# Second-stage convolved projections in fp32r parts with three banks, and a mixer output turned tile by tile

## The chip, the cores and the metric

The kernel runs on one core of one Trainium2 chip (trn2). The metric is device microseconds from start to end of one launch; the table further down gives the median of several. All stages follow one another inside this launch: five engines (TensorE, VectorE, ScalarE, GpSimd, SyncE) run their own instruction queues and meet at semaphores.

## The reference

256 tokens of width 1024 pass through two stacks. The first has two layers, each of feed-forward, hybrid mixer, feed-forward:

```python
for l in range(DEPTH):                        # DEPTH = 2
    h = swiglu(rms_norm(x, ...), w_gate, w_up, w_down); x = x + 0.5 * rms_norm(h, ...)
    h = hybrid_mixer(rms_norm(x, ...), ...);            x = x + rms_norm(h, ...)
    h = swiglu(rms_norm(x, ...), ...);                  x = x + 0.5 * rms_norm(h, ...)
# inside hybrid_mixer: sparse attention (its blocks are xb below: keys plus a position code),
# a short convolution u = cg * xc, and at the end
merged = concatenate([rms_norm(attn, ...), rms_norm(conv, ...)]); return merged @ w_out
```

The second has one layer. Its first step projects a context `hc` and the tokens `h` (both 256 x 1024), and runs a convolution of 5 taps and a silu over the projected channels:

```python
pc = hc @ w_in[:, :OFF_CF]
xb_c = silu(dwconv_centred(pc[..., :XB_CH], conv_w[:, :XB_CH], conv_b[:XB_CH]))
dtc = softplus(pc[..., OFF_DT:OFF_CF] + dt_bias)
p = h @ w_in
xl = silu(dwconv_centred(p[..., :XB_CH], ...)); cl = silu(dwconv_centred(p[..., OFF_CF:OFF_Z], ...))
```

Then come a state-space scan, a Fourier mix, gates, and a mixture of 32 experts over all tokens.

## The kernel before

**Products.** In the first stack and from the scan on, a product of fp32 numbers is made of three fp32r products: the weights and the inputs are each split into a high part (rounded to fp32r) and a low part (the rest), and hi·hi, hi·lo and lo·hi are added up in a bank of PSUM. The weights come in chunks through a ring of three slots of 128x4096, filled by transfers that SyncE issues in the order in which the chunks are used. A chunk is split in two halves of 128x2048. ScalarE writes a half's high part into one of four buffers (`act_split`, a CAST at L381), VectorE the low part into `ring_lo` (`dve_split`, a TENSOR_TENSOR at L390), and TensorE waits for both. A slot is filled again when TensorE has used the halves in it (`half_used`).

**The second stage's projections** (`pe_projections`, `act_projections`, `dve_projections`, about 1088 us to 1320 us) are the exception. They consist of 56 blocks `n` of 128 channels; blocks 0 to 23 are of the context, the rest of the tokens. The weights stay whole (fp32): four blocks share a chunk of 512 channels, and a block is 8 matmuls of 128x256 (L1780), which the profile counts as 16. The results go to bank `n % 2`. For each block VectorE takes the first tap and the bias out of PSUM (L1829), then adds four taps (L1834); ScalarE applies silu (L1804); TensorE turns the block (two transposes, L1794), and ScalarE copies the turned block out of PSUM (L1819). Eight of the 56 (kind C) are not turned. TensorE starts block `n` when the taps of block `n - 2` are done:

```python
pe.wait_ge(*(at("tap", n - 2) if n >= 2 else at("hout", self.before, 0, n)))
for k in range(KD):
    mm = pe.matmul(bank[n % 2][:, 0:SEQ], w[:, k, j * P:(j + 1) * P], self.conv_src(n)[:, k, :], ...)
```

Around the blocks stand: `pe_dt(0)` ahead of block 0 and `pe_dt(1)` ahead of block 24 (the step widths `dt`, 32 small matmuls, L1845); `act_softplus` ahead of ScalarE's part of blocks 0 and 24 (L1863 to L1869, two of its steps with a table load of their own); `pe_cumsum` behind blocks 1 and 25 (L1856, L1857); the normed and turned tokens `x1` at blocks 1 to 7 (L1745 and others); and `dve_xw_ctx` at blocks 14, 18, 22 and 26 (L1961, eight 128x512 products by twos for each). The high part of the tokens (`hx`) is made by ScalarE at block 50, the low part by VectorE behind block 55 (L2034).

**The last feed-forward of the first stack** ends with its down projection and the joint (`act_joint`, `dve_joint`, L641, L665, L671), which adds the normed result to `x`. The projections' block 0 waits there for `hout`, the point where VectorE has read banks 0 and 1.

**The mixers** run twice (for layer 0 from about 200 us to 362 us). `xb` is made on VectorE (L1486, 8 operations) behind `dve_u` (L1538) and `dve_max` (L1409, L1412), and TensorE's `pe_compress` (L1167) waits for it. At the end, the attention's output `o` is scaled (L1528 for tile 1, L1531 for tile 0), turned in two halves of four channel blocks with both tiles in each (`pe_turn_o`, `act_turn_half`, `dve_turn_half`, L1399), and multiplied by the last two halves of `w_out` (`pe_last`, L415). The joint and the next feed-forward's first turns (L608) follow.

## Time and profile before

| what | us |
|---|---|
| median of 3 runs | 2609.37 (2603.39 to 2612.96) |
| the profiled execution, its own time | 2603.46 |
| span of its core in the profile | 2602.0 |
| mean granted clock of TensorE | 0.995 of full speed |
| TensorE busy | 98% of the span |
| VectorE, ScalarE, GpSimd busy | 42%, 33%, 4% |
| experts (about 1650 us to the end), TensorE's work | over a third of the span |

The busy shares are of the whole span. Stages differ: in the experts VectorE and ScalarE have a tenth of the time to do, in the first stack and the projections half of it or more. "Own time" is what was measured for the execution that was profiled; it is 5.9 us below the median of the runs. Times below that look like `1138.72` are microseconds from the start of the span.

### The profile page before, as it was taken

The numbers are of one execution on the slowest core, as the hardware profiler recorded it, in microseconds if no ns is written. First come the engines' busy times: TensorE is split into PE (matmuls) and PEld (weight loads), VectorE is DVE, ScalarE is ACT, GpSimd is POOL, SyncE is SP. The second block draws the span as 40 slices with busy tenths as digits, with TensorE's granted clock in tenths as the row PEclk, the third lists the DMA queues.
The fourth block names the chain that finished last, engine by engine and source line by source line (L and its number), as shares of the span: only waits on it lengthen the run. The fifth ranks groups of instructions, "written<-read, shape, count | busy, mean of one in ns | idle before, by whom it ended". The sixth has DMA issues, their size and how long they took to land.

```text
span 2602.0 us, 31966 instructions
## 1 busy us (share of the span) xinstructions
PE 2554.2 (98%) x13032; PEld 1712.8 (66%) x13032; DVE 1093.5 (42%) x1710; ACT 854.0 (33%) x1357; POOL 100.5 (4%) x139
## 2 busy tenths in 40 slices
PE   8999999999999999999999999999999999999998
PEld 6888678888887688888878878544444444444443
DVE  5545565555464655476665636311111111111111
ACT  5435454444454454323144644211111111111111
POOL 1000210000002100000000000000000000000000
PEclk9999999999999999999999999999999999999999
DMA  7556655555565665424322336899999999999996
GB/s 261 180 175 208 239 204 190 182 198 181 175 216 196 233 223 186 158 102 158 134 81 82 113 119 212 322 425 430 431 431 431 431 431 431 431 431 432 431 431 257
DMA packets 69389, 688.45 MB, mean 265 GB/s; under 512 B 7906, under 2 KB 8050, under 8 KB 11920
## 3 DMA queue, kind: packets, MB, share of 16 engines
q1 hardware_dynamic: 66368, 676.27, 66.4%
q0 software_dynamic: 2928, 10.87, 1.3%
q8 instruction: 67, 1.10, 0.2%
q14 instruction: 26, 0.21, 0.0%
HBM read 683.98 MB, written 1.05 MB: 263 GB/s over the span
## 4 chain that ended last, share of the span: by engine, by line
PE 96%; DVE 2%; ACT 1%; DMA 0%; issue 0%; POOL 0%; SPq 0%; DVEq 0%; ACTq 0%
PE bank L415 39%; PE bank L2748 26%; PE bank L1780 7%; PE bank L2695 4%; PE bank L2762 2%; PE bank L2738 2%; PE bank L452 1%; PE bank L2113 1%; PE bank L2091 1%; PE bank L720 1%; PE bank L1045 1%; PE bank L1167 1%; DVE ring_r L390 1%; PE bank L1237 1%; PE bank L1016 1%; PE bank L455 1%
## 5 line engine op out<-in xcount | busy, mean ns | idle before, releaser
L390 DVE TENSOR_TENSOR ring_r<-ring,split_r 128x2048 fp32r<-128x2048 f32 (+1 forms) x200 | 451.6, 2284 | 340.5 <-ACT split_r L381 340.3
L415 PE MATMUL bank<-split_r,xT_r 128*128 128x512 f32 (+1 forms) x1760 | 548.0, 389 | 6.4 <-DVE xT_r L1399 5.4
L381 ACT CAST split_r<-ring 128x2048 fp32r<-128x2048 f32 (+1 forms) x200 | 375.1, 1902 | 153.2 <-PE bank L415 124.2
L415 PE MATMUL bank<-split_r,work_r 128*128 128x512 f32 x1280 | 409.6, 396 | 0.5 <-DVE ring_r L390 0.5
L415 PEld LDWEIGHTS bank<-split_r,xT_r 128*128 128x128 f32 x1760 | 330.2, 189 | 75.7 <-DVE xT_r L1399 5.8
L2748 PE MATMUL bank<-ring,work 128*64 128x512 f32 x1536 | 342.1, 594 | 1.7 <-DVE work L2712 1.7
L415 PE MATMUL bank<-ring_r,xT_r 128*128 128x512 f32 (+1 forms) x880 | 340.4, 387 | 0.0
L415 PEld LDWEIGHTS bank<-split_r,work_r 128*128 128x128 f32 x1280 | 240.3, 188 | 54.3 <-issue 3.3
L2748 PEld LDWEIGHTS bank<-ring,work 128*64 128x64 f32 x1536 | 107.1, 137 | 228.6 <-issue 228.6
L415 PE MATMUL bank<-ring_r,work_r 128*128 128x512 f32 x640 | 249.2, 389 | 0.0
L2748 PE MATMUL bank<-split,work 128*64 128x512 f32 x1024 | 232.2, 595 | 0.0
L1780 PE MATMUL bank<-work,ring 128*128 128x256 f32 x896 | 200.9, 379 | 0.0
L415 PEld LDWEIGHTS bank<-ring_r,xT_r 128*128 128x128 f32 x880 | 166.2, 189 | 32.2
L1780 PEld LDWEIGHTS bank<-work,ring 128*128 128x128 f32 x896 | 166.9, 190 | 23.1 <-issue 1.0
L2785 ACT ACTIVATE work<-work 128x512 f32<-128x512 f32 x32 | 20.1, 629 | 467.5 <-DVE work L2796 467.5
L2748 PEld LDWEIGHTS bank<-split,work 128*64 128x64 f32 x1024 | 70.5, 137 | 130.2 <-issue 128.0
L415 PEld LDWEIGHTS bank<-ring_r,work_r 128*128 128x128 f32 x640 | 120.3, 188 | 27.8 <-issue 4.1
L2695 PE MATMUL bank<-work 128*128 128x64 f32 x1056 | 121.7, 274 | 0.5 <-DVE work L2719 0.5
L2695 PEld LDWEIGHTS bank<-work 128*128 128x128 f32 x1056 | 120.5, 192 | 0.7 <-DVE work L2719 0.7
L2798 DVE TENSOR_SCALAR work<-bank 128x512 f32<-128x512 f32 x32 | 22.1, 691 | 234.6 <-PE bank L2762 234.6
L2748 PE MATMUL bank<-work 128*64 128x512 f32 x512 | 115.3, 592 | 0.0
L2796 DVE TENSOR_SCALAR work<-bank 128x512 f32<-128x512 f32 x32 | 22.1, 691 | 217.8 <-PE bank L2762 217.8
(369 smaller groups left out, 2281.8 us busy)
## 6 DMA issues: line engine op xcount, KB each, us to landing
ring<-in_stream SPq DMA_DIRECT2D x256, 1024.0 KB, 5.0
ring<-in_stream SPq DMA_DIRECT2D x96, 2048.0 KB, 14.0
split<-in_stream SPq DMA_DIRECT2D x64, 2048.0 KB, 13.5
work<-in_stream SPq DMA_DIRECT2D x32, 2048.0 KB, 11.3
row<-in_rows POOLq DMA_DIRECT2D x6, 512.0 KB, 4.4
ring<-in_stream SPq DMA_DIRECT2D x4, 560.0 KB, 4.6
work<-in_conv POOLq DMA_DIRECT2D x2, 768.0 KB, 5.8
x<-in_x SPq DMA_DIRECT2D x1, 1024.0 KB, 10.1
```

The lines of the kernel that those rows point to most:

```text
L381: act.copy(hi, self.part(half, self.ring)).then_inc(*up("half_hi", half.h))
L390: dve.tensor_tensor(self.part(half, self.ring_lo), self.part(half, self.ring), hi.bitcast(F32), ALU.subtract).then_inc(*up("half_lo", half.h))
L415: mm = self.nc.tensor.matmul(out, a[x][a_at], w[y][w_at], start=start and n == 0, stop=stop and n == 2)
L452: pe.matmul(out, self.xT[0][:, 4 * j + k, tokens], w[y][:, k], start=4 * j + k + y == 0, stop=False)
L455: mm = pe.matmul(out, self.xT[1][:, 4 * j + k, tokens], w[0][:, k], start=False, stop=4 * j + k == KD - 1)
L720: tr = pe.transpose(self.bank[b][:, j * SEQ + m * P:j * SEQ + (m + 1) * P], self.hid[i % 2][:, m, (j2 + j) * P:(j2 + j + 1) * P], self.ident)
L1016: mm = pe.matmul(bank[2 * (i % 2) + hh % 2][:, c0:c0 + P], self.qT[1][r, h // 2, m * P:(m + 1) * P], self.kT[r, 2 * b + g, kb * P:(kb + 1) ...
L1780: mm = pe.matmul(bank[n % 2][:, 0:SEQ], w[:, k, j * P:(j + 1) * P], self.conv_src(n)[:, k, :], start=(k == 0), stop=(k == KD - 1))
L2695: mm = pe.matmul(bank[k // 4][:, k * SLOTS:(k + 1) * SLOTS], self.xs[:, m, k * P:(k + 1) * P], self.Pm[:, m, :], start=(m == 0), stop=(m = ...
L2738: mm = self.nc.tensor.matmul(self.bank[4 + 2 * m + h][:, :], self.PT[rows, m * P:(m + 1) * P], self.yb[rows, :], start=False, stop=stop)
L2748: mm = self.nc.tensor.matmul(self.bank[bank][h * SLOTS:(h + 1) * SLOTS, :], lhsT(k0 + k), w[:, k, h * 512:(h + 1) * 512], start=start and ...
L2762: mm = pe.matmul(bank[part][h * SLOTS:(h + 1) * SLOTS, :], self.sel[0:N_EXP, :], self.bias[0:N_EXP, part * D + h * 512:part * D + (h + 1) ...
```

## The change

There are two parts. In **the projections of the second stage**, the 56 blocks take their weights and their inputs in high and low parts: 24 matmuls of 128x256 a block instead of 8, all fp32r. The chunks of weights are laid out so that one half holds two blocks, so 28 halves more pass through `act_split` and `dve_split`, one at every even `n`. The context is split too (`act_context_hi`, `dve_context_lo`), during the last feed-forward, and `hx` now at blocks 13 and 15. The blocks go to three banks, and TensorE waits for the taps of block `n - 3`. The first tap moves from VectorE to ScalarE (`act_conv_first`). `pe_dt(0)` moves into the last feed-forward's `pe_last`, and `pe_dt(1)` from block 24 to block 12.

In **the mixers**, `xb` is made ahead of `dve_u` and `dve_max`, and the output is turned one tile of tokens at a time, tile 1 first; the joint and the next feed-forward take tile 1 first as well.

```diff
         x_c, dt_c, bf_c, cf_c, bb_c, cb_c = [n_mod + c for c in range(4)], *(n_mod + c for c in range(4, 9))
-        for c in (dt_c, bf_c, bb_c, *x_c, dt_c, bf_c, cf_c, bb_c, cb_c, *x_c):
+        for i, c in enumerate((dt_c, bf_c, bb_c, x_c[0], dt_c, *x_c[1:], bf_c, cf_c, bb_c, cb_c, *x_c)):
             w = 2 * NH2 if c == dt_c else 512
-            self.add_chunk(t["stream2"][c, :, 0:KD * w], KD, w, False)
-        self.n_slots = RING - 1
+            self.add_chunk(t["stream2"][c, :, 0:KD * w], KD, w, c != dt_c, c != dt_c)
+            self.n_slots = RING - 1
+        self.first_piece = len(self.halves)
...
         if split:
             n = 2 if kt * width > HALF else 1
             for j in range(n):
-                half = Half(len(self.halves), kt // n, width, chunk, j)
+                half = Half(len(self.halves), kt if by_column else kt // n, width // n if by_column else width, chunk, j)
...
         if self.last_ffn:
             self.dve_split(3)
             self.dve_context_turned()
-            self.dve_split(KF // 2 - 5)
+            self.dve_split(KF // 2 - 7)
+            self.dve_context_lo()
+            self.dve_split(2)
         else:
             self.dve_split(KF // 2 - 2)
...
@@ -1099,10 +1113,8 @@
             if i >= 2:
                 self.pe_mod_turn(st, i - 2)
         self.pe_out_u(st, 1)
-        self.pe_turn_o(st)
-        for j in range(2):
-            pe.wait_ge(*at("turn_lo", (st, "o"), j))
-        self.out_done = self.pe_last(self.xT, 0, st, lambda k: None)
+        self.out_done = self.pe_last(self.xT, 0, st, lambda m, k: None if k else ("turn_lo", (st, "o"), m),
+                                     lambda: self.pe_turn_o(st, 0))
...
+            elif i == 7:
+                self.act_split(2)
             if i == 3:
                 act.wait_ge(*at("conv", st))
                 act.wait_ge(*at("zeroed", st, 3))
                 self.act_rstd((st, "u"), self.u, 512, 6)
...
-        for m, col in ((1, 5), (0, 4)):
-            act.wait_ge(*at("o", st, m))
-            act.wait_ge(*self.s.last("sum_sq"))
-            act.activation(self.squares[:, 0:512], self.o[:, m, :], ACT.Square, scale=512 ** -0.5,
-                           accum_out=self.stat[:, col:col + 1]).then_inc(*up("sum_sq", (st, "o"), m))
-            self.act_split(1)
-        self.act_turn_half((st, "o"), 0)
+        self.act_o_squares(st, 0)
+        self.act_turn_o(st, 1)
+        self.act_turn_o(st, 0)
         self.act_split(2)
         self.act_joint(st, self.out_done, 1.0)
...
@@ -1470,12 +1519,6 @@
         dve.wait_ge(*last("att_step"))
         dve.reciprocal(self.gates, self.gates).then_inc(*up("att_step"))
 
-        dve.wait_ge(*at(*self.xc_done))
-        dve.wait_ge(*at("z", st, 3, 1))
-        self.dve_u(st, 0)
-        self.dve_u(st, 1)
-        self.dve_max(st, 1)
-        self.dve_max(st, 0)
         dve.wait_ge(*at("kc2", st, 1))
         dve.wait_ge(*at("zeroed", st, 3))
         for kv in range(2):
@@ -1486,6 +1529,12 @@
                     i = dve.tensor_tensor(self.xb[kv][:, 8 * jh:8 * jh + 8, g, 0:N_CMP], v[:, :, jh:jh + N_CMP, 0],
                                           spread(pe_cols[:, 8 * jh:8 * jh + 8], 2, N_CMP), ALU.add)
         i.then_inc(*up("xb", st))
+        dve.wait_ge(*at(*self.xc_done))
+        dve.wait_ge(*at("z", st, 3, 1))
+        self.dve_u(st, 0)
+        self.dve_u(st, 1)
+        self.dve_max(st, 1)
+        self.dve_max(st, 0)
...
+            if i == 7:
+                self.dve_o_scaled(st, 1)
+                self.dve_split(2)
...
-        dve.wait_ge(*at("rstd", (st, "o"), 1))
-        dve.tensor_scalar(self.o[:, 1, :], self.o[:, 1, :], self.stat[:, 5:6], None, ALU.mult).then_inc(*up("o_scaled", st, 1))
-        self.dve_split(1)
-        dve.wait_ge(*at("rstd", (st, "o"), 0))
-        dve.tensor_scalar(self.o[:, 0, :], self.o[:, 0, :], self.stat[:, 4:5], None, ALU.mult).then_inc(*up("o_scaled", st, 0))
-        self.dve_split(1)
-        self.dve_turn_half((st, "o"), 0)
+        self.dve_turn_o(st, 1)
+        self.dve_o_scaled(st, 0)
+        self.dve_turn_o(st, 0)
         self.dve_split(2)
...
     def conv_src(self, n):
-        return self.src[0] if n < 24 else self.src[1]
+        return self.cx if n < 24 else self.hx
+
+    def conv_bank(self, n):
+        return self.bank[(0, 1, 4)[n % 3]]
 
     def conv_turns(self, n):
         return self.blocks[n][0] != "C"
 
     def conv_at(self, n):
 
-        return self.raw_at(self.conv_chunk[n]) if self.blocks[n][2] == 3 else self.s.at("conv_mm", n)
+        return self.s.at("half_used", self.conv_half[n]) if n % 2 else self.s.at("conv_mm", n)
...
-        pe.wait_ge(*(at("tap", n - 2) if n >= 2 else at("hout", self.before, 0, n)))
+        pe, at, up = self.nc.tensor, self.s.at, self.s.up
+        if n % 2 == 0:
+            self.conv_now = self.pe_take()
+        half, w = self.conv_now
+        self.conv_half[n] = half.h
+        if n >= 2:
+            pe.wait_ge(*(at("tap", n - 3) if n >= 3 else at("cx_lo", 0)))
+        else:
+            pe.wait_ge(*at("hout", self.before, 0, n))
+        if n == 8:
+            pe.wait_ge(*at("turn_even", "x1", 1))
...
+        x, cols = self.conv_src(n), slice(n % 2 * P, (n % 2 + 1) * P)
         for k in range(KD):
-            mm = pe.matmul(bank[n % 2][:, 0:SEQ], w[:, k, j * P:(j + 1) * P], self.conv_src(n)[:, k, :],
-                           start=(k == 0), stop=(k == KD - 1))
-        mm.then_inc(*(self.raw_up(ch.c) if j == 3 else up("conv_mm", n)))
+            for i, (y, z) in enumerate(((0, 0), (0, 1), (1, 0))):
+                mm = pe.matmul(self.conv_bank(n)[:, 0:SEQ], w[y][:, k, cols], x[z][:, k, :], start=k == 0 and i == 0,
+                               stop=k == KD - 1 and i == 2)
+        mm.then_inc(*(up("half_used", half.h) if n % 2 else up("conv_mm", n)))
         if n >= 2 and self.conv_turns(n - 2):
             self.pe_conv_turn(n - 2)
...
+    def act_conv_first(self, n):
+        act, at, up = self.nc.scalar, self.s.at, self.s.up
+        wt = self.conv_w[:, self.blocks[n][3]]
+        act.wait_ge(*self.conv_at(n))
+        if n >= 3:
+            act.wait_ge(*at("conv_turned" if self.conv_turns(n - 3) else "conv_silu", n - 3))
+        act.activation(self.acc[n % 3], self.conv_bank(n)[:, 0:SEQ], ACT.Identity, scale=wt[:, 2:3],
+                       bias=wt[:, 5:6]).then_inc(*up("tap_first", n))
+
...
@@ -1821,16 +1909,13 @@
     def dve_conv(self, n):
         dve, at, up, last = self.nc.vector, self.s.at, self.s.up, self.s.last
         kind, a, j, block = self.blocks[n]
-        acc, src, wt = self.acc[n % 3], self.bank[n % 2], self.conv_w[:, block]
-        dve.wait_ge(*self.conv_at(n))
-        if n >= 3:
-            dve.wait_ge(*(at("conv_turned", n - 3) if self.blocks[n - 3][0] in ("Bc", "Xc", "X")
-                          else at("conv_silu", n - 3)))
-        dve.tensor_scalar(acc, src[:, 0:SEQ], wt[:, 2:3], wt[:, 5:6], ALU.mult, ALU.add).then_inc(*up("tap"))
+        acc, src, wt = self.acc[n % 3], self.conv_bank(n), self.conv_w[:, block]
+        dve.wait_ge(*at("tap_first", n))
         for tap in (0, 1, 3, 4):
             s = tap - 2
             to = acc[:, max(0, -s):SEQ - max(0, s)]
-            dve.wait_ge(*last("tap"))
+            if tap:
+                dve.wait_ge(*last("tap"))
             dve.scalar_tensor_tensor(to, src[:, max(0, s):SEQ - max(0, -s)], wt[:, tap:tap + 1], to, ALU.mult,
...
     def pe_projections(self):
         pe, at = self.nc.tensor, self.s.at
-        pe.wait_ge(*at("turn_even", "ctx", 5))
-        pe.wait_ge(*at("turn_odd", "ctx", 7))
-        self.pe_dt(0)
         for n in range(56):
-            if n == 24:
+            if n == 12:
                 pe.wait_ge(*at("turn_even", "x1", 5))
                 pe.wait_ge(*at("turn_odd", "x1", 7))
...
+            self.act_conv_first(n)
+            if n:
+                self.act_conv(n - 1)
+            if n >= 3 and self.conv_turns(n - 3):
+                self.act_conv_turn(n - 3)
+            if n % 2 == 0:
+                self.act_split(1)
...
+            elif n == 13:
+                act.wait_ge(*at("turn_odd", "x1", 7))
                 act.copy(self.hx[0], self.src[1]).then_inc(*up("hx_hi", 0))
...
                 self.dve_dt_raw(n // 24)
             self.dve_conv(n)
+            if n % 2 == 0:
+                self.dve_split(1)
             if n in (0, 24):
                 self.dve_dt_step(n // 24)
...
-        dve.wait_ge(*at("hx_hi", 0))
-        dve.tensor_tensor(self.hx[1], self.src[1], self.hx[0].bitcast(F32), ALU.subtract).then_inc(*up("hx_lo", 0))
+            elif n == 15:
+                dve.wait_ge(*at("hx_hi", 0))
+                dve.wait_ge(*self.raw_at(self.dt_chunk[1]))
+                dve.tensor_tensor(self.hx[1], self.src[1], self.hx[0].bitcast(F32), ALU.subtract).then_inc(*up("hx_lo", 0))
```

(The layout of the weights, which the host writes, puts two times 256 channels behind one another. The renamed banks of `pe_dt`, the moves of `z`, and the ring's sync in the experts are left out here.)

On SyncE, which issues the transfers, the second stage's chunks began like this before:

```order
L348 DMA ring<-in_stream 128x512 [waits raw_used]
L348 DMA ring<-in_stream 128x2048 [waits raw_used] x16
```

and begin like this now:

```order
L347 DMA ring<-in_stream 128x512 [waits half_used]
L353 DMA ring<-in_stream 128x2048 [waits half_used] x2
L353 DMA ring<-in_stream 128x2048 [waits raw_used] x2
L353 DMA ring<-in_stream 128x2048 [waits half_used] x2
```

(the 128x512 is the weights of the second `dt`; before it the same stood for the first). A transfer now waits for a half's use by its own slot's last chunk. The stage has two slots instead of three, since the third holds the tokens; in the planner's order the chunk of blocks 12 to 15 goes into the slot of blocks 8 to 11, and so its halves wait for those of blocks 8, 9 and 10, 11.

On ScalarE, among the blocks that are turned, this stood before (line, operation, output <- input, what it waits for):

```order
L1804 ACTIVATE work<-work 128x256 [waits second_dve]
L1819 COPY work<-bank 128x2x128 [waits second_pe]
```

and this stands there now, for two blocks (the piece repeats):

```order
L1884 ACTIVATE work<-bank,work 128x256 [waits second_pe]
L1892 ACTIVATE work<-work 128x256 [waits second_dve]
L1907 COPY work<-bank 128x2x128 [waits second_pe]
L380 CAST split_r<-ring 128x2048 [waits half_used,dma_ring1_1]
L1884 ACTIVATE work<-bank,work 128x256 [waits second_pe,half_used]
L1892 ACTIVATE work<-work 128x256 [waits second_dve]
L1907 COPY work<-bank 128x2x128 [waits second_pe]
L1884 ACTIVATE work<-bank,work 128x256 [waits second_pe]
L1892 ACTIVATE work<-work 128x256 [waits second_dve]
```

L1884 is the first tap, which was VectorE's; L1892 is the silu of the block before it, L1907 the turned block of two earlier still. The CAST of a half stands behind them once in two blocks. On VectorE, at the same place, before:

```order
L1829 TENSOR_SCALAR work<-bank,work 128x256 [waits second_pe]
L1834 SCALAR_TENSOR_TENSOR work<-bank,work 128x254 [waits second_dve]
L1834 SCALAR_TENSOR_TENSOR work<-bank,work 128x255 [waits second_dve] x2
L1834 SCALAR_TENSOR_TENSOR work<-bank,work 128x254 [waits second_dve]
```

and now, again for two blocks:

```order
L1919 SCALAR_TENSOR_TENSOR work<-bank,work 128x254 [waits second_act]
L1919 SCALAR_TENSOR_TENSOR work<-bank,work 128x255 [waits second_dve] x2
L1919 SCALAR_TENSOR_TENSOR work<-bank,work 128x254 [waits second_dve]
L389 TENSOR_TENSOR ring_r<-ring,split_r 128x2048 [waits half_hi]
L1919 SCALAR_TENSOR_TENSOR work<-bank,work 128x254 [waits second_act]
L1919 SCALAR_TENSOR_TENSOR work<-bank,work 128x255 [waits second_dve] x2
L1919 SCALAR_TENSOR_TENSOR work<-bank,work 128x254 [waits second_dve]
```

The first tap is gone from VectorE; its four taps wait for ScalarE's, and a subtraction that waits for the CAST of the same half (`half_hi`) stands between two blocks. At the end of a mixer VectorE had this:

```order
L1528 TENSOR_SCALAR work<-work,stat 128x512 [waits rms_pool]
L390 TENSOR_TENSOR ring_r<-ring,split_r 128x2048 [waits half_hi]
L1531 TENSOR_SCALAR work<-work,stat 128x512 [waits rms_pool]
L390 TENSOR_TENSOR ring_r<-ring,split_r 128x2048 [waits half_hi]
L1399 SCALAR_TENSOR_TENSOR xT_r<-bank,cols,xT_r 128x256 [waits turn_hi]
L1399 SCALAR_TENSOR_TENSOR xT_r<-bank,cols,xT_r 128x256
L1399 SCALAR_TENSOR_TENSOR xT_r<-bank,cols,xT_r 128x256 [waits turn_hi]
L1399 SCALAR_TENSOR_TENSOR xT_r<-bank,cols,xT_r 128x256
L390 TENSOR_TENSOR ring_r<-ring,split_r 128x2048 [waits half_hi] x2
L665 TENSOR_TENSOR work<-bank,row 128x512 [waits post_sq,dma_row]
```

and has this now:

```order
L1418 SCALAR_TENSOR_TENSOR xT_r<-bank,cols,xT_r 128x128 [waits turn_hi]
L1418 SCALAR_TENSOR_TENSOR xT_r<-bank,cols,xT_r 128x128 x3
L1425 TENSOR_SCALAR work<-work,stat 128x512 [waits rms_pool]
L1418 SCALAR_TENSOR_TENSOR xT_r<-bank,cols,xT_r 128x128 [waits turn_hi]
L1418 SCALAR_TENSOR_TENSOR xT_r<-bank,cols,xT_r 128x128 x3
L389 TENSOR_TENSOR ring_r<-ring,split_r 128x2048 [waits half_hi] x2
L668 TENSOR_TENSOR work<-bank,row 128x512 [waits post_sq,dma_row]
```

The scaling of tile 1 and two subtractions have moved ahead of this piece, into the attention's last unit, and the turned output (now L1418) comes by tiles; the last two subtractions still stand right ahead of the joint (L665, now L668).

## Rows read from the trace of the kernel before

**Rows 1.** The page's first part: busy time, share of the span, instructions.

```profile
PE 2554.2 (98%) x13032; PEld 1712.8 (66%) x13032; DVE 1093.5 (42%) x1710; ACT 854.0 (33%) x1357; POOL 100.5 (4%) x139
```

**Rows 2.** Windows: span, busy PE, PEld, DVE, ACT, POOL, clock, DMA share, GB/s.

```profile
1088.00:1320.00 232.00, 228.97 (x1119) 195.08 (x1117) 159.17 (x327) 68.74 (x149) 8.26 (x11) 1.00 0.35 133
264.00:268.00 4.00, 3.34 (x20) 1.56 (x22) 2.06 (x4) 4.00 (x6) 0.59 (x1) 0.70 0.49 114
350.90:354.30 3.40, 2.75 (x7) 2.20 (x8) 3.02 (x4) 2.70 (x2) 0.00 (x0) 0.51 0.24 99
```

**Rows 3.** Timeline of one projection block: start, us, engine, line, idle before.

```profile
1138.72 0.54 DVE L1829 TENSOR_SCALAR work<-bank,work 128x256 f32<-128x256 f32 x1 [1.06 <-PE bank L1780]
1138.74 3.62 PE L1780 MATMUL bank<-work,ring 128*128 128x256 f32 x16
1138.94 0.37 ACT L1819 COPY work<-bank 128x256 f32<-128x256 f32 x1 [0.83 <-PE bank L1794]
1139.30 2.04 DVE L1834 SCALAR_TENSOR_TENSOR work<-bank,work 128x254 f32<-128x254 f32 x4
1141.37 0.42 ACT L1804 ACTIVATE work<-work 128x256 f32<-128x256 f32 x1 [2.06 <-DVE work L1834]
1142.42 3.62 PE L1780 MATMUL bank<-work,ring 128*128 128x256 f32 x16
```

**Rows 4.** The page's fifth part: groups of the two splits and of weight loads.

```profile
L390 DVE TENSOR_TENSOR ring_r<-ring,split_r 128x2048 fp32r<-128x2048 f32 (+1 forms) x200 | 451.6, 2284 | 340.5 <-ACT split_r L381 340.3
L381 ACT CAST split_r<-ring 128x2048 fp32r<-128x2048 f32 (+1 forms) x200 | 375.1, 1902 | 153.2 <-PE bank L415 124.2
L415 PEld LDWEIGHTS bank<-split_r,xT_r 128*128 128x128 f32 x1760 | 330.2, 189 | 75.7 <-DVE xT_r L1399 5.8
```

**Rows 5.** Chain and timeline: fp32r matmuls of 280 and of 256 columns.

```profile
227.08 6.16 PE bank L415 x48
1644.57 1.68 PE L2531 MATMUL bank<-work_r 128*128 128x256 f32 x12
```

**Rows 6.** Lines by form, window 1088 to 1318 us, VectorE and ScalarE.

```profile
L1961 DVE TENSOR_TENSOR work<-work 128x512 f32<-128x512 f32 x16 | 9.9, 683 | 0.0
...
L1804 ACT ACT_TABLE_LOAD x4 | 5.1, 1283 | 0.1
```

**Rows 7.** Timeline of the projections' start and end.

```profile
1086.62 1.34 DVE L665 TENSOR_TENSOR work<-bank,row 128x512 f32<-128x512 f32 x2 [15.54 <-ACT work L641]
1088.36 3.68 PE L1845 MATMUL bank<-ring,work 128*128 128x64 f32 x32
1092.38 0.28 DVE L1884 TENSOR_TENSOR work<-bank,work 128x128 f32<-128x128 f32 x1
1092.70 0.31 ACT L1863 ACTIVATE work<-work 128x128 f32<-128x128 f32 x1 [2.74 <-DVE work L1884]
1098.23 0.42 ACT L1804 ACTIVATE work<-work 128x256 f32<-128x256 f32 x1 [0.53 <-DVE work L1834]
1318.82 0.42 ACT L1804 ACTIVATE work<-work 128x256 f32<-128x256 f32 x1 [2.06 <-DVE work L1834]
```

**Rows 8.** The page's sixth part: transfers, KB each, us from issue to landing.

```profile
ring<-in_stream SPq DMA_DIRECT2D x256, 1024.0 KB, 5.0
```

**Rows 9.** TensorE's waits: us in total, times, longest.

```profile
PE bank L1167 <- DVE work L1486: 7.4, 2, 3.7
PE bank L415 <- DVE xT_r L1399: 5.4, 2, 2.7
```

**Rows 10.** Timeline of the first mixer, around xb and around its end.

```profile
266.54 5.57 DVE L390 TENSOR_TENSOR ring_r<-ring,split_r 128x2048 fp32r<-128x2048 f32 x2 [1.94 <-ACT split_r L381]
276.12 0.50 PE L415 MATMUL bank<-split_r,xT_r 128*128 128x512 f32 x1
351.83 4.49 DVE L390 TENSOR_TENSOR ring_r<-ring,split_r 128x2048 fp32r<-128x2048 f32 x2 [0.38 <-ACT split_r L381]
359.43 1.34 DVE L665 TENSOR_TENSOR work<-bank,row 128x512 f32<-128x512 f32 x2 [3.10 <-ACT work L641]
```

180 lines of the change are left out of this document (118 added, 62 removed).

## The prediction

> **What bounds the kernel now.** I began with the page's first part and with windows by stage. TensorE is busy 98% of the whole [rows 1], so in the mean only work taken off TensorE, or its waits, can count; but a stage can change hands. In the projections TensorE is busy 228.97 of 232.00 us, VectorE 159.17 and ScalarE 68.74, at full clock [rows 2]. A timeline of one block then shows the order: a block starts every 3.68 us [rows 3], of which 3.62 are its sixteen matmul records; VectorE needs 0.54 + 2.04 and waits 1.06 for TensorE; ScalarE needs 0.42 + 0.37. TensorE sets the pace there, and the other two follow. The reader should see that the slack is 1.1 us on VectorE and 2.9 on ScalarE for each block. In the mixers I read TensorE's waits: two rows stand out that the change touches, 3.7 us for `xb` and 2.7 us for the turned output, once in each of two mixers [rows 9].
>
> **TensorE's side of the projections.** The new block has 24 fp32r matmuls of 256 columns. Forty-eight of 280 columns took 6.16 us, 0.128 each, so 0.117 for 256; twelve of exactly 256 columns took 1.68, 0.140 each with the pipeline's end [rows 5]. I take 0.118: 24 are 2.84, and with the turns (3.68 − 3.46 = 0.22, where 3.46 is the period without turns) 3.06. That is 0.6 us less than now. Over 56 blocks it would be 35 us, if TensorE went on setting the pace. A load of weights is on record with 0.189 [rows 4]; if none lay beside a matmul, a block would take 24 × (0.118 + 0.189) = 7.4. The 0.128 and 0.140 are whole matmuls with their loads, so they speak against that. [...]
>
> **What is added.** One half now holds two blocks. A half costs ScalarE a cast of 1.902 us and VectorE a subtraction of 2.284 [rows 4], 28 times each. ScalarE also gets the first tap: bounded by 0.37 (a copy of 128x256 out of PSUM) and 0.54 (VectorE's) [rows 3]; I take 0.50, since it has a scale and a bias. VectorE gives 0.54 away.
>
> **The pace after it.** Sums per pair of blocks: TensorE 6.1; VectorE 2 × 2.04 + 2.29 = 6.4; ScalarE 2 × (0.50 + 0.42 + 0.37) + 1.90 = 4.5. None of these is the pace, because the queues hook into each other. In the new order ScalarE's cast stands behind the silu of block n − 1 and a copy, and the silu waits for the taps of n − 1. VectorE's subtraction waits for that cast, and the taps of n + 1 stand behind the subtraction. So from the end of one odd block's taps to the next: silu 0.42, copy 0.37, cast 1.90, subtraction 2.29, four taps 2.04, and hand-overs (1141.37 − 1139.30 − 2.04 = 0.03 each, four to five) 0.13. Sum **7.15 us a pair, 3.58 a block**. The taps of block n lie beside the cast (2.04 of 0.42 + 0.37 + 1.90 + 0.06 = 2.75, VectorE waits about 0.7). Before, a pair took 7.36. The whole gain of the fp32r matmuls shrinks to 0.2 us a pair, and TensorE waits a microsecond in each.
>
> **The start.** Before, block 0's taps ended at 1098.2 [rows 7]. Now `pe_dt(0)` (3.5 us of the 3.68 [rows 7], moved, not saved) stands inside the feed-forward's last product, so TensorE is through that at 1092.0 instead of 1088.4. VectorE has the context's low part (2.28, as a half of the same shape [rows 4]) and two subtractions (4.6) ahead of the joint: with `dt` there at about 1086.6, it is free at 1093.5. The joint takes 1092.4 − 1086.6 = 5.8 less 0.4 of waiting (now the squares are done), up to 1099.0; `dt`'s bias 0.3; then ScalarE's softplus 3.7 (1092.70 to 1096.40, two table loads of 1.28 in it), which stood beside matmuls and now stands ahead of the first tap; first tap 0.5; taps 2.04. Block 0's taps end at 1105.7: **+7.5**.
>
> **From there to the last taps.** Before 1318.8 − 1098.2 = 220.6 [rows 7]. Now 27.5 pairs × 7.15 = 196.6. To this I add what doesn't fit in the pair's 0.7 of slack, by following the four queues block after block with these durations (the same hand count for the order of before ends at 1319.1, the trace at 1318.8):
> - blocks 0 to 8: `pe_cumsum(0)`, behind the late softplus, stands ahead of block 2; two further table loads (1.28 [rows 6]) and the squares of x: +9.0;
> - blocks 8 to 12: the transfer. The half of blocks 12, 13 can't be issued before block 9's matmuls end, since it goes into that slot; it lands 5.0 us later [rows 8], then come its cast and subtraction, which VectorE's queue waits for although block 10's taps could go. Twice, 7 + 5 less the slack: +10.6;
> - blocks 14 to 22: two `dve_xw_ctx` (a quarter of 9.9 each [rows 6]) and the tokens' low part 2.28, on VectorE, which had room before: +7.4;
> - blocks 22 to 30: two more `xw` 5.0, the second softplus with 4.2 ahead of block 24's first tap, and the cumsum that waits for it ahead of block 26's matmuls, with two table loads behind, 8.1: +17.3;
> - the rest −0.9 (in the blocks of kind C there is no turn).
>
> Together 240.0: **+19.4**. TensorE's waits also cost clock: after a wait of 2.7 us the window's granted clock is 0.51 over 3.4 us, after the 3.7 us one 0.70 over 4 us [rows 2], so 1.2 to 1.7 us each. In the new stage there are four or five waits of 4 to 9 us, by my count: **+6.5**. Behind the stage, unit 0 gets the tokens' low part (2.28) and the first split earlier: **−1**. Projections: 7.5 + 19.4 + 6.5 − 1 = **+32.4**. With all durations 10% off, the stage's end moves from 1334 to 1351.
>
> **The mixers.** `xb`: TensorE's wait of 3.7 goes, with the 1.2 of clock. But VectorE's two subtractions, from 266.54 to 272.11, end no sooner than ScalarE's casts allow; the product that needs them (276.12) can move to 272.15 at best [rows 10]. **−4.0** each (bounds 0 and −5.5). Output: TensorE's wait of 2.7 and its slow stretch (1.6) go. Then the joint is late next: its first operation stands at 359.43 behind 3.1 us of waiting, and VectorE's two subtractions (from 351.83, 4.5 us) now stand behind the eight smaller turns, and end at about 358.8 [rows 10]. **−1.0** each (bounds −4.3 and +2). Two mixers: **−10** (0 to −20).
>
> **Sum.** 32.4 − 10 = 22.4, less 1 for feed-forwards whose first tile comes earlier: 21.4 by the execution's own 2603.5, so 2625. The median of the runs is 5.9 above that execution: **2631**. What this kernel's measurement can tell from no change is 0.5%, 13 us.
>
> **The rivals.**
> - *The mixers give all.* With both waits and both slow stretches gone, −10 a mixer: 32.4 − 20 − 1 = +11, 2621. For it: the waits are plain in rows 9. Against: VectorE's subtractions in rows 10.
> - *The cast hides.* If ScalarE reached the cast before the taps end (it has 2.6 us of slack a pair), VectorE alone would set 6.45 a pair. 27.5 × 0.7 = 19 less, and with a queue that runs ahead the dips (6.5) and a part of the transfer's wait (some 4) less: 32.4 − 19 − 10 − 10 − 1 = −8, 2602. For it: all sums per engine allow it. Against: the silu ahead of the cast waits for taps.
> - *TensorE stays the pace* (the other side). If splits ran two halves ahead all the time, 3.06 a block: 56 × 0.6 = −35, with the mixers −45, 2564. It decides as soon as the pair's chain is under 6.1. For it: the halves have four buffers, and the second stage's VectorE was 31% idle. Against: 6.4 of VectorE's own work a pair is more than 6.1 already.
> - *Weight loads don't overlap*: 7.4 a block, 56 × 3.7 = +207 less the mixers' 10, 2806. Against: rows 5. [...]
>
> **Chances.** Forecast 0.60, full mixers 0.13, hidden cast 0.12, TensorE 0.10, loads 0.03; 0.02 for others. The likeliest one's own range is 2618 to 2645. The range of 8 in 10 leaves TensorE and the loads out, and reaches from the hidden cast, 2602, to the upper end, 2646. Slower than +13 us (2622) comes with most of the forecast and the loads, 0.60; within 13 us with the full mixers and most of the hidden cast, 0.26; faster with TensorE and the rest of it, 0.14.
>
> **What would show it.** The first taps would start every 3.6 us in pairs of uneven length, and VectorE's subtraction would wait for ScalarE's cast some 0.7 us in each; TensorE would have a wait of a microsecond for each pair, on the low part or on taps. At blocks 0, 10, 12, 24 and 26 waits of 4 to 9 us. Block 0's silu at about 1096 to 1098 after the mixers' 10 are taken off, the last one near 1342. In the mixers L1167's wait is gone, and the matmuls behind it start 4 us sooner. I would be wrong if ScalarE's first tap took 0.8 instead of 0.5 (+8 in all), if the transfer's wait is not there, or if the subtractions ran ahead of the taps.

## The result and the profile after

| what | before | after |
|---|---|---|
| median of 4 runs | 2609.64 (2603.39 to 2612.96) | 2635.24 (2633.54 to 2636.84) |
| own time of the profiled execution | 2603.46 | 2635.03 |
| span | 2602.0 | 2633.7 |

The ratio is 1.0102, 95% interval 1.0088 to 1.0116: the change made the kernel slower by 1.0%. Forecast were 2631 and slower by more than 0.5%. The page's first part answers to [rows 1]:

```profile
PE 2546.0 (97%) x13480; PEld 1723.0 (65%) x13480; DVE 1128.8 (43%) x1691; ACT 930.1 (35%) x1450; POOL 100.7 (4%) x139
```

TensorE has 8 us less to do and takes 32 us longer for it. Windows over the projections, which now last from about 1081 to 1349 us (columns as in [rows 2]), say where:

```profile
1081.00:1110.00 29.00, 20.66 (x123) 19.16 (x122) 18.63 (x24) 16.23 (x25) 5.13 (x6) 0.82 0.41 146
1130.00:1170.00 40.00, 32.87 (x260) 32.13 (x258) 23.57 (x37) 18.62 (x33) 0.00 (x0) 0.91 0.37 130
1230.00:1265.00 35.00, 29.96 (x186) 26.26 (x186) 21.40 (x37) 17.45 (x29) 0.00 (x0) 0.82 0.21 67
1300.00:1340.00 40.00, 36.90 (x303) 36.03 (x304) 35.37 (x54) 24.23 (x41) 4.11 (x4) 1.00 0.47 159
```

TensorE was busy 99% there before, at full clock; now it is idle 3 us in 40 where the stage runs steadily, and 5 to 8 us in 29 to 40 where it doesn't, with the granted clock down to 0.82. What it waits for stands in the view of its waits (us in total, times, longest):

```profile
PE bank L1875 <- ACT work L1907: 20.7, 14, 4.9
PE bank L610 <- DMA x<-in_x: 12.5, 1, 12.5
PE bank L1941 <- DVE work L1982: 10.8, 2, 6.4
PE bank L610 <- DVE x L674: 6.5, 2, 3.3
PE bank L2028 <- DVE work L2046: 5.8, 3, 3.0
```

L1875 is the turn of a block, which stands for the turned copy (L1907) of an earlier one; L1941 is the cumsum behind softplus; L610 are the first turns of `x` for a feed-forward, a wait that has taken the place of the one for the turned output. The two of [rows 9] are gone.

The chain that ended last, cut to one steady pair of blocks (start, us, what; pieces under 0.1 us are left out but the silu's), shows the pace:

```profile
1306.69 0.22 issue
1306.90 0.35 ACT work L1907
1307.26 1.82 ACT split_r L380
1309.10 2.29 DVE ring_r L389
1311.39 0.40 DVE work L1919
1311.82 0.49 DVE work L1919
1312.34 0.49 DVE work L1919
1312.86 0.49 DVE work L1919
1313.37 0.03 ACT work L1892
1313.48 0.22 issue
1313.70 0.35 ACT work L1907
```

No piece of TensorE is in it. It reads: copy, cast, subtraction, four taps, silu (L1892), and again. The silu's piece is short because the rest of it stands as "issue": its record starts at 1306.58, and its 0.42 overlap the copy's start. One round takes 1313.70 − 1306.90 = 6.80 us. The trap of the transfer at block 10 stands in the timelines of VectorE and ScalarE:

```profile
1139.18 2.04 DVE L1919 SCALAR_TENSOR_TENSOR work<-bank,work 128x254 f32<-128x254 f32 x4
1148.52 2.29 DVE L389 TENSOR_TENSOR ring_r<-ring,split_r 128x2048 fp32r<-128x2048 f32 x1 [7.30 <-ACT split_r L380]
1150.73 3.98 DVE L1919 SCALAR_TENSOR_TENSOR work<-bank,work 128x254 f32<-128x254 f32 x8
1161.63 2.29 DVE L389 TENSOR_TENSOR ring_r<-ring,split_r 128x2048 fp32r<-128x2048 f32 x1 [6.92 <-ACT split_r L380]
```

```profile
1146.59 1.90 ACT L380 CAST split_r<-ring 128x2048 fp32r<-128x2048 f32 x1 [6.88 <-DMA ring<-in_stream]
1159.70 1.90 ACT L380 CAST split_r<-ring 128x2048 fp32r<-128x2048 f32 x1 [6.22 <-DMA ring<-in_stream]
```

VectorE stands 7 us for a cast that itself stands for its transfer, twice. At the end of the first mixer (VectorE and TensorE, answering to [rows 10]) the joint is late:

```profile
355.68 4.50 DVE L389 TENSOR_TENSOR ring_r<-ring,split_r 128x2048 fp32r<-128x2048 f32 x2 [0.67 <-ACT split_r L380]
360.09 1.28 DVE L668 TENSOR_TENSOR work<-bank,row 128x512 f32<-128x512 f32 x2
```

```profile
362.09 1.12 PE L610 MATMUL bank<-consts,x 128*128 128x128 f32 x4 [3.25 <-DVE x L674]
```

### The profile page after: what moved, and what is told of

Its sections match the earlier page's. It is cut to its first block, busy times and chain, and to the rows that moved or that the text cites. A ratio compares the mean times of both kernels' runs of the same rounds, so it can differ in the third digit from the quotient of the medians.

```text
span 2633.7 us, 32981 instructions
## 1 busy us (share of the span) xinstructions
PE 2546.0 (97%) x13480; PEld 1723.0 (65%) x13480; DVE 1128.8 (43%) x1691; ACT 930.1 (35%) x1450; POOL 100.7 (4%) x139
## 4 chain that ended last, share of the span: by engine, by line
PE 88%; DVE 6%; ACT 4%; issue 1%; DMA 1%; POOL 0%; SPq 0%; ACTq 0%; DVEq 0%
PE bank L414 38%; PE bank L2840 25%; PE bank L2787 4%; DVE ring_r L389 3%; PE bank L2854 2%; PE bank L2830 2%; PE bank L1861 2%; ACT split_r L380 2%; PE bank L452 1%; DVE work L1919 1%; PE bank L2186 1%; PE bank L2208 1%; PE bank L729 1%; PE bank L1059 1%; PE bank L2028 1%
## 5 line engine op out<-in xcount | busy, mean ns | idle before, releaser
L389 DVE TENSOR_TENSOR ring_r<-ring,split_r 128x2048 fp32r<-128x2048 f32 (+1 forms) x228 | 515.5, 2284 | 370.6 <-ACT split_r L380 370.4
L380 ACT CAST split_r<-ring 128x2048 fp32r<-128x2048 f32 (+1 forms) x228 | 428.6, 1903 | 180.7 <-PE bank L414 120.3
L414 PE MATMUL bank<-split_r,work_r 128*128 128x512 f32 x960 | 301.7, 392 | 0.5 <-DVE ring_r L389 0.5
L414 PEld LDWEIGHTS bank<-split_r,work_r 128*128 128x128 f32 x960 | 180.8, 188 | 38.3 <-DVE ring_r L389 0.9
L414 PE MATMUL bank<-ring_r,work_r 128*128 128x512 f32 x480 | 187.3, 390 | 0.0
L1919 DVE SCALAR_TENSOR_TENSOR work<-bank,work 128x254 f32<-128x254 f32 x224 | 106.5, 481 | 37.9 <-ACT work L1884 31.8
L2879 ACT COPY work<-bank 128x256 f32<-128x256 f32 x32 | 11.9, 372 | 286.2 <-PE bank L2861 286.2
L414 PE MATMUL bank<-split_r,ring_r 128*128 128x512 f32 x320 | 109.0, 412 | 0.0
```

The lines of the kernel that those rows point to most:

```text
L380: act.copy(hi, self.part(half, self.ring)).then_inc(*up("half_hi", half.h))
L389: dve.tensor_tensor(self.part(half, self.ring_lo), self.part(half, self.ring), hi.bitcast(F32), ALU.subtract).then_inc(*up("half_lo", half.h))
L414: mm = self.nc.tensor.matmul(out, a[x][a_at], w[y][w_at], start=start and n == 0, stop=stop and n == 2)
L1919: dve.scalar_tensor_tensor(to, src[:, max(0, s):SEQ - max(0, -s)], wt[:, tap:tap + 1], to, ALU.mult, ALU.add).then_inc(*(up("tap", n) if t ...
```

## The experiments

Each is an edit of the changed kernel if nothing else is said. "Last taps" are those of block 55; where two traces are compared, they are counted from block 0's taps. Two measures are used: the median of the runs, and the trace of one execution.

### The two parts apart

`p_only` puts the mixers back, `m_only` is the kernel before with the mixers' part, `xb_only` the kernel before with this alone:

```diff
+        (xb: 8 operations of VectorE, then_inc xb)
         dve.wait_ge(*at(*self.xc_done))
         dve.wait_ge(*at("z", st, 3, 1))
         self.dve_u(st, 0)
...
         self.dve_max(st, 0)
-        (xb)
```

> The projections' part of the change alone, with the mixers as before. Theory: the parts add up; the changed kernel is at 2635.2 and the mixers' part alone gave 9, so 2642 to 2645 (the prediction's own term for the projections was +32.4, which is 2642). Rival: the mixers and the projections are coupled, through the tile order and the joint, and this runs at 2635 to 2639.

> The kernel before with the mixers' part of the change alone (xb sooner, output tile by tile, tile 1 first); the projections stay fp32 in two banks. My theory, from the changed kernel's trace: xb gives 3.9 us a mixer, the output about 1.4 up to the next feed-forward's first turn, and the low clock behind TensorE's new wait of 3.3 us for the joint takes 1.6 back, so some 3.7 a mixer and up to 7.4 in all, or 2.5 if the first mixer again loses 5 to a low clock: 2601 to 2607 by the median of the runs. Rival, the term of the prediction: 10 us for both, 2600. Second rival: the mixers' part is worth nothing or costs, and all of the 26 us is not the projections' alone: 2610 or more.

> The kernel before with xb ahead of dve_u and dve_max, and nothing else. Theory, the prediction's term: TensorE's wait of 3.7 us goes, and the matmuls that need VectorE's two subtractions start 3.8 to 4.0 us sooner in each mixer, 8 in all: 2601. The output's new order is then worth about 1 for the two mixers (the mixers' part alone ran at 2599.9). Rival: the wait moves on in full to the subtractions, and xb gives under 4 in all: 2605 or more, and the output's order is worth 5.

Measured, with the ratio to the kernel before:

| kernel | median | ratio, 95% interval |
|---|---|---|
| `p_only` | 2639.54 | 1.0119 (1.0102 to 1.0136) |
| `m_only` | 2599.91 | 0.9973 (0.9961 to 0.9984) |
| `xb_only` | 2603.05 | 0.9984 (0.9975 to 0.9994) |

The projections cost 30.6 us (2639.54 − 2608.9), the mixers give 9.1 (2609.0 − 2599.91). The prediction had 32.4 and 10. My revised reading before the run, that the mixers give at most 7.4, fell. `p_only` lies between its theory (from 2642) and its rival (up to 2639), nearer to the rival. The sum is 21.5 and the whole change 25.6, so 4 us are left over. The three intervals are 3 to 4 us wide to each side, so this may be no more than their spread, and the clock in the mixers is another place where it can lie (last section); a coupling of the two parts isn't shown. Of the 9.1, `xb` gives 6.0, between its theory (8) and its rival (under 4). The output's new order is worth 3.1 by the medians, with intervals that overlap. By the traces, from the start of the product with `w_out`'s second half of the convolution's rows to the next feed-forward's second chunk of gate and up weights, it is worth nothing: 35.4 us before (granted clock 0.95), 35.5 in `m_only`, and 34.1 in `xb_only`, whose clock was 1.00 there. Which of the two holds stays open.

### Is TensorE's work what counts? `t_less`

```diff
-            for i, (y, z) in enumerate(((0, 0), (0, 1), (1, 0))):
+            for i, (y, z) in enumerate(((0, 0), (1, 0))):
```

> The changed kernel with two of the three fp32r products of the 56 blocks (the product of the weights' high part with the inputs' low part is left out), all splits, casts and waits as they are. That takes 56 x 8 x 0.12 = 54 us of work off TensorE. Theory (the chain of silu, copy, cast, subtraction and taps sets the pace, TensorE only waits in it): under a tenth of it shows, where TensorE's blocks stand behind the cumsum or a transfer, 2628 to 2637. Rival: TensorE still sets much of the pace, and 20 us or more come off: 2615 or less.

2625.89, 9.3 us less, for an estimated 54 us of work. From block 32's last tap to block 54's it took 1334.0 − 1260.2 = 73.8 us here and 1342.8 − 1269.0 = 73.8 in the changed kernel: the same. VectorE's timeline in it has the waits of the changed kernel:

```profile
1314.05 2.29 DVE L389 TENSOR_TENSOR ring_r<-ring,split_r 128x2048 fp32r<-128x2048 f32 x1 [0.60 <-ACT split_r L380]
1316.26 3.98 DVE L1919 SCALAR_TENSOR_TENSOR work<-bank,work 128x254 f32<-128x254 f32 x8
1320.85 2.43 DVE L389 TENSOR_TENSOR ring_r<-ring,split_r 128x2048 fp32r<-128x2048 f32 x1 [0.61 <-ACT split_r L380]
```

So TensorE isn't the pace in the steady part at all, as forecast. The 9 us come from ahead of block 30 (8.7 by the traces, 3.5 of them in blocks 22 to 30), where TensorE follows a cumsum or a transfer; that is more than the 7 at most that I expected.

### The chain and the transfer: `e_cast`, `e_slot`, `c_slotcast`

`e_cast` moves the cast:

```diff
             self.act_conv_first(n)
+            if n % 2 == 0:
+                self.act_split(1)
             if n:
                 self.act_conv(n - 1)
             if n >= 3 and self.conv_turns(n - 3):
                 self.act_conv_turn(n - 3)
-            if n % 2 == 0:
-                self.act_split(1)
```

> The changed kernel with one move: ScalarE's cast of a half stands ahead of the silu and the turned copy instead of behind them. Theory (the pair of blocks is a chain silu, copy, cast, subtraction, taps): the cast no longer waits for taps, the pair falls from 6.8 to 7.1 us to VectorE's own sum of 6.3, and VectorE's waits for the cast go where the weights are there; at blocks 8 to 12 the silu now stands behind the cast that waits for its transfer, which takes some of it back. Net 5 us sooner at the last taps, about 2630. Rival: VectorE's or TensorE's own work is already the pace, and a pair stays at 6.8: no change, 2635.

2635.21, no change, where 5 us less were expected. The theory of the pace held all the same: blocks 32 to 54 took 1341.1 − 1273.0 = 68.1 us instead of 73.8, 6.2 a pair instead of 6.7. But the price at the transfer was larger than I had put it: from block 10's taps to block 12's 21.7 us instead of 13.1, and from block 8's to block 12's 37.9 instead of 26.6. ScalarE's timeline shows why:

```profile
1144.37 1.90 ACT L380 CAST split_r<-ring 128x2048 fp32r<-128x2048 f32 x1 [7.50 <-DMA ring<-in_stream]
1146.17 0.41 ACT L1892 ACTIVATE work<-work 128x256 f32<-128x256 f32 x1
...
1152.49 0.56 ACT L1884 ACTIVATE work<-bank,work 128x256 f32<-128x256 f32 x1 [4.62 <-PE bank L1861]
1160.28 1.90 ACT L380 CAST split_r<-ring 128x2048 fp32r<-128x2048 f32 x1 [7.22 <-DMA ring<-in_stream]
```

The silu (L1892) and the copy (L1907) are stuck behind the waiting cast, TensorE's turn waits 7.6 us for that copy, and the next transfer's slot only comes free when TensorE goes on. `e_slot` takes that wait away; the second `dt`'s weights go into the unused half of the third slot (in the planner's loop, with the same offset in the transfer and in `pe_take_raw`):

```diff
+            if i == 4:
+                chunk = Chunk(len(self.chunks), t["stream2"][c, :, 0:KD * w], KD, w, 2, self.in_slot[2])
+                chunk.at_half = 1
...
+                continue
```

> The changed kernel with the weights of the second dt in the free half of the third slot, so that the weights of blocks 12 to 15 go into the slot of blocks 4 to 7 and are issued after block 5 instead of block 9. Theory (the transfer sets the pace at blocks 8 to 12): ScalarE's two casts there, which stood 6.9 and 6.2 us for the transfer, no longer wait, and the last taps end 11 us sooner, 2624. Rival: the wait only hid another one, as for the low parts or the state products behind it, and under 4 us come out: 2631 or more.

2620.31: 14.9 less, where 11 were expected; by the traces 231.5 us from the first taps to the last instead of 244.9, 13.4 less. The cast at the same place:

```profile
1144.75 0.42 ACT L1902 ACTIVATE work<-work 128x256 f32<-128x256 f32 x1 [0.49 <-DVE work L1929]
1145.08 0.36 ACT L1917 COPY work<-bank 128x256 f32<-128x256 f32 x1
1145.33 1.90 ACT L388 CAST split_r<-ring 128x2048 fp32r<-128x2048 f32 x1
```

No wait. With both edits:

> Both moves of the last two projection experiments together: the transfer's slot freed, and ScalarE's cast ahead of the silu and the copy. Theory: the cast alone gave nothing in all because the six us that it saved in blocks 28 to 54 (a pair there took 6.1 instead of 6.75) went back at blocks 10 to 12, where the silu then stood behind a cast that waited for its transfer. With the transfer in time both count: 13 us less than with the slot alone (2620), so 2607. Rival: the two gains are the same waits counted twice, and only 3 to 6 us come out: 2614 to 2617.

2612.57 by the median of runs that reach from 2606.16 to 2614.8: 7.7 less than the slot alone. By the traces the stage gained 231.5 − (1319.5 − 1097.4) = 9.4. Both gains count, but not in full: between theory (13) and rival (3 to 6).

### The first tap: `v_first`

```diff
-            self.act_conv_first(n)
...
-        dve.wait_ge(*at("tap_first", n))
+        (wait for the block's matmuls and for the turn of n - 3)
+        dve.tensor_scalar(acc, src[:, 0:SEQ], wt[:, 2:3], wt[:, 5:6], ALU.mult, ALU.add).then_inc(*up("tap"))
```

> The changed kernel with the first tap back on VectorE (0.54 us ahead of the four taps), ScalarE without it. Theory: VectorE's taps of an odd block lie in the chain, so 0.54 per pair is added, and where VectorE was free ahead of them it is hidden: +8 to +15, 2643 to 2650. Rival: ScalarE's first tap was itself in the chain with its hand-over, and moving it back costs nothing: 2635.

2638.79, 3.6 more. In the steady part the theory holds: blocks 32 to 54 took 1347.3 − 1266.5 = 80.8 us instead of 73.8, +0.64 a pair. But block 0's taps came sooner, since VectorE doesn't wait for ScalarE's softplus: 188.3 us behind the last feed-forward's second chunk of weights instead of 192.0. So ScalarE's first tap is worth 9 us over the stage and costs 4 at its start; the net lies between the rival (nothing) and the theory (8 or more).

### The mixers' end: `o_fix`, `m_ofix`

```diff
         self.act_turn_o(st, 1)
+        self.act_split(1)
         self.act_turn_o(st, 0)
-        self.act_split(2)
+        self.act_split(1)
...
         self.dve_o_scaled(st, 0)
+        self.dve_split(1)
         self.dve_turn_o(st, 0)
-        self.dve_split(2)
+        self.dve_split(1)
```

> The changed kernel with one cast and one subtraction of a half moved from behind the turn of tile 0 to ahead of it, at the end of both mixers. Theory (the joint is late because VectorE's last two subtractions stand right ahead of it, until 360.1, while the squares are there at 358.0): the joint starts 2 us sooner in each mixer, TensorE's wait of 3.3 us for the new x shrinks to about 1.3, and less clock is lost behind it: 4 to 7 us in all, 2629 to 2631. Rival: the moved cast makes the turn of tile 0 later, and TensorE waits there instead: no change or slower.

> The mixers' part alone (fp32 projections), with one cast and one subtraction ahead of the turn of tile 0 at the mixers' ends. Theory: the joint's lateness is a matter of the mixers and not of the projections, so the same 6 to 7 us come off as from the changed kernel: 2593. It also says what a good fp32r stage has to beat. Rival: a part of the 7 us was luck of the clock in the first mixer (up to 5 us differ from run to run there), and 2 to 4 come off: 2596 to 2598.

2628.03, 7.2 less, a little over the 4 to 7 expected, and from `m_only` 2595.55, 4.4 less, where the theory had 6 to 7 and the rival 2 to 4. From the turn of tile 1 to the next feed-forward's second chunk of weights the traces with this edit have 29.0 us in both mixers, those with the changed order 32.7 or 32.8: 3.8 a mixer, 7.6 for the two. That `m_ofix` shows less of it by its median stays open; the clock of the first mixer (last section) moves a single kernel by as much. TensorE's waits for the new `x` are down from 6.5 us in two to 2.1. One subtraction is left ahead of the joint:

```profile
351.79 2.29 DVE L389 TENSOR_TENSOR ring_r<-ring,split_r 128x2048 fp32r<-128x2048 f32 x1 [0.67 <-ACT split_r L380]
354.00 1.28 DVE L668 TENSOR_TENSOR work<-bank,row 128x512 f32<-128x512 f32 x2
```

### All of it, and a version that beats both: `c_all`, `c_best`

`c_all` is `c_slotcast` with `o_fix` and with softplus behind block 0's and 24's first tap and cast. `c_best` also draws the steps of `dt` apart:

```diff
-            if n in (1, 25):
+            if n in (3, 27):
                 self.pe_cumsum(n // 24)
...
-            elif n in (2, 26):
+            if n in (4, 28):
                 self.act_dt(n // 24)
...
-            if n in (0, 24):
+            if n in (1, 25):
                 self.dve_dt_step(n // 24)
-            elif n in (2, 26):
+            elif n in (3, 27):
                 self.dve_dt_ends(n // 24)
-            elif n in (3, 27):
+            elif n in (5, 29):
                 self.dve_dt_last(n // 24)
```

> As the run with slot and cast, and two more moves: softplus stands behind the first tap and the cast of blocks 0 and 24 instead of ahead of them, and the end of the mixers has one cast and one subtraction ahead of the turn of tile 0. Theory: softplus no longer holds the first taps (4 us at block 0, 4 at block 24), and the mixers' end gives the 7 us that it gave alone: 2592 to 2596. Rival: the step that follows softplus on VectorE and the cumsum behind it on TensorE hold block 2 and block 26 anyway, so softplus gives 1 us and not 8: 2599 to 2601.

> The run with slot, cast, softplus and mixers' end, and the steps of dt drawn apart: VectorE's step one block later, TensorE's cumsum behind block 3 instead of 1, what follows it at blocks 3 to 5, and the same behind block 24. Theory: the queues no longer stop for each other at blocks 2 and 26, where TensorE still waited 4 us each for the step, a turn and a copy; following the queues, the last taps end 10 to 12 us sooner than there (2597): 2585 to 2588. Rival: VectorE's own sum (6.3 a pair and some 22 us beside the blocks) already fills the stage, and at most 3 us come off: 2594 or more.

`c_all` 2597.14 (ratio 0.9964, 0.9950 to 0.9978), `c_best` **2581.28** (ratio 0.9896, 0.9880 to 0.9913), 28 us below the kernel before and 14 below `m_ofix`, the best version with fp32 projections. `c_all` came out between its theory (up to 2596) and its rival (from 2599), `c_best` 4 us below the lower end of its theory. `c_all` had almost the stage of before (215.7 us from the first taps to the last instead of 220.6, and a later start). Its queues still stopped for each other at blocks 2 and 26. In `c_best` the same takes 204.6. The gain is where the edits are: blocks 22 to 30 took 48.0 us in `c_slotcast`, 41.2 with softplus behind the first tap, and 35.5 with the steps of `dt` drawn apart; blocks 0 to 8 took 38.7 in `c_all` and 33.3 in `c_best`. VectorE waits for nothing in the steady part:

```profile
1249.59 3.97 DVE L1931 SCALAR_TENSOR_TENSOR work<-bank,work 128x254 f32<-128x254 f32 x8
1253.48 2.28 DVE L397 TENSOR_TENSOR ring_r<-ring,split_r 128x2048 fp32r<-128x2048 f32 x1
1255.68 3.98 DVE L1931 SCALAR_TENSOR_TENSOR work<-bank,work 128x254 f32<-128x254 f32 x8
1259.57 2.28 DVE L397 TENSOR_TENSOR ring_r<-ring,split_r 128x2048 fp32r<-128x2048 f32 x1
```

6.09 us a pair (1259.57 − 1253.48), all of it VectorE's work. But TensorE has as much to do: from block 32's taps to block 54's it is busy 67.9 of 68.1 us, VectorE 65.8, and the mean pair is 6.2. The stage is even between the two.

## Why the prediction was right, and where it was off

**TensorE's side.** 0.118 a matmul was forecast; a block took 3.12 with its last record's tail, or 24 starts 0.12 apart:

```profile
1319.80 0.28 PE L1861 MATMUL bank<-ring_r,split_r 128*128 128x256 f32 x1
1319.92 0.28 PE L1861 MATMUL bank<-ring_r 128*128 128x256 f32 x1
1320.04 0.40 PE L1861 MATMUL bank<-ring_r,split_r 128*128 128x256 f32 x2
1320.28 0.28 PE L1861 MATMUL bank<-ring_r 128*128 128x256 f32 x1
```

Each has a load of weights of its own on record, of 0.19 us (1344 loads for the 56 blocks); two of three bring other weights than the matmul before had, since the high part is used twice in a row. With starts 0.12 apart the loads lie beside the matmuls. The Trainium skill ("TensorE: Matmul & The Clock Gate", Part 3, The mechanism) says that they do so only where the row group differs; this trace, with all matmuls over the whole 128x128 array, disagrees. The same page of the Trainium skill (Part 2, Step-by-step, on the load of weights) also allows a load ahead into a background buffer; that would fit, but no run here shows the buffer.

**The stage.** By the traces, us between taps, forecast as base plus surplus:

| blocks | forecast | measured |
|---|---|---|
| block 0's taps, against before | +7.5 | +6.7 |
| 0 to 8 | 28.6 + 9.0 = 37.6 | 38.2 |
| 8 to 12 (transfer) | 14.3 + 10.6 = 24.9 | 26.6 |
| 12 to 22 | 35.75 + 7.4 = 43.2 | 43.7 |
| 22 to 30 (second softplus) | 28.6 + 17.3 = 45.9 | 51.1 |
| 30 to 55 | 89.4 − 0.9 = 88.5 | 85.2 |
| TensorE's low clock | 6.5 | in the rows above |
| behind the last taps, against before | −1 | +2.7 |

From the first taps to the last it is 244.9 against 246.5 forecast. The pace of 7.15 a pair was 5 to 7% too much (6.5 to 7.0 were measured from block 32 on, 6.7 in the mean): instructions of one engine overlap at their ends, so eight taps take 3.98 and not 4.08, and silu with copy 0.6 and not 0.79. Blocks 22 to 30 cost 5 more; `c_all` and `c_best` show how much of that stretch was softplus and the steps of `dt`. Behind the last taps −1 was forecast for work that VectorE has done sooner, and +2.7 came. Part of it is clock: TensorE waits 3.7 us ahead of the last turn instead of 2.7, and in the 6 us behind the last taps the granted clock is 0.50 (windows of the kernel before, then of the changed one):

```profile
1318.80:1324.80 6.00, 5.00 (x23) 4.39 (x24) 5.01 (x2) 5.64 (x11) 2.67 (x2) 0.72 0.67 280
1347.80:1353.80 6.00, 4.60 (x18) 4.07 (x19) 0.73 (x2) 3.88 (x10) 2.55 (x2) 0.50 0.00 0
```

Another 1.3 us went 301 us further on, where 5 us ran at 0.66 in the changed kernel and at 1.00 before. The first tap took 0.56, not 0.50. That the chain, and not TensorE, sets the pace, is shown by `t_less` and `e_cast`; the transfer by `e_slot`.

**The mixers.** −10 was forecast for the two, −9.1 measured in `m_only`. `xb`: TensorE's product behind the two subtractions stood 3.9 us sooner in both mixers, counted from their first turns, where 4.0 was forecast. In the first:

```profile
261.49 7.10 PE L1186 MATMUL bank<-ring,work 128*32 128x256 f32 x64
...
272.87 0.47 PE L414 MATMUL bank<-split_r,xT_r 128*128 128x512 f32 x1 [1.53 <-DVE ring_r L389]
```

The wait of 3.7 has become one of 1.5 for the subtraction. The output's −1 was forecast because the joint would be late at 358.8 instead of 359.4; it was late at 360.1, and with TensorE's wait of 3.3 us and the low clock behind it the part came to nothing by the trace.

**The sum.** The change of the medians was forecast with +21.4 and measured with +25.6. In the two profiled executions it was larger, +31.6, so 10 us are missing there:

| term | forecast | profiled pair |
|---|---|---|
| up to the last feed-forward's second chunk (mixers, first tiles) | −11 | −1.9 |
| from there to block 0's taps | +7.5 | +6.7 |
| first taps to last, with the low clock | +25.9 | +24.3 |
| behind the last taps | −1 | +2.7 |

The mechanism of the projections came out in its terms. The gap is in the mixers: they took 178.4 and 173.5 us against 177.2 twice before, 2.6 less in all and not 10. `xb` gave its 3.9 in each; the first mixer lost 5 us to TensorE's clock (last section), and the output's new order gave nothing.

The 5.9 us by which the profiled execution of before lay under its median are not a constant of the measurement: the changed kernel's profiled execution lies 0.2 under its own. `p_only`, with the code of before in the mixers, took 179.1 and 179.6 us for them, 4 us more in all, so executions of one code differ there by most of that amount. Adding the 5.9 was right in effect, because it compares median with median, and it brought the forecast to 4 us below the result. There was luck in that closeness too: by the medians of the two parts the projections cost 1.8 less than forecast and the mixers, with the 1 us for the first tiles, gave 1.9 less, which cancels. The 4 us left are those by which the two parts don't add up to the whole.

## What to carry to other kernels

When a product moves to a cheaper form that needs splits on other engines, the sums per engine don't tell the pace: write down in queue order what each engine waits for, and follow it once around; here every engine had slack and the round did not. A cast placed behind a short step that waits is worth moving ahead of it, but only once its own input is always there, since in a strict queue it passes its wait on to everything behind it. And where a scarce slot is taken by a small chunk, look at which transfer has to wait for it.

## What the runs showed of the hardware

The mixers' code is the same in `m_only`, the changed kernel, `e_cast`, `e_slot` and `c_slotcast`, and yet from the first turns of `x` to the next feed-forward's second chunk of weights the first mixer took 176.7, 178.4, 176.7, 178.1 and 173.5 us, the second 173.4 or 173.5 in all five. `t_less` and `v_first`, with the same mixers, had 178.3 and 173.6, and 173.5 and 178.0: the long one can be the second too. What differs is TensorE's granted clock, in stretches in which TensorE had no wait at all; from the changed kernel and from `c_slotcast` (window 300 to 310):

```profile
300.00:310.00 10.00, 10.00 (x64) 7.34 (x63) 4.70 (x12) 3.73 (x14) 0.09 (x1) 0.66 0.42 162
```

```profile
300.00:310.00 10.00, 10.00 (x87) 7.03 (x85) 6.49 (x19) 4.10 (x15) 1.16 (x2) 0.88 0.59 219
```

Busy 10.00 of 10.00 in both, at 0.66 and 0.88 of full speed. In this part TensorE works on many small matmuls. Up to 6 us for each mixer turn on this (`xb_only` had 176.8 and 170.4 for the same code), which is as much as what the mixers' edits give; so such edits are judged by medians, and a single trace tells where the time went only after its clock was read. What decides when the clock falls there was not tested.

VectorE's subtraction of a half takes 2.28 us in 25 of the 28 that `c_best` has between 1085 and 1300 us. The other three took 2.79 to 2.90, and they are the three beside which GpSimd works on a pair of 128x512 multiplications, as here (VectorE, then GpSimd):

```profile
1265.66 2.81 DVE L397 TENSOR_TENSOR ring_r<-ring,split_r 128x2048 fp32r<-128x2048 f32 x1
```

```profile
1265.28 4.10 POOL L2154 TENSOR_TENSOR work<-work 128x512 f32<-128x512 f32 x2 [165.03 <-ACT work L1919]
```

That is half a microsecond in a pair of blocks whose pace VectorE helps to set. No run moved the multiplications, so that they are the cause isn't tested.
